# Recurrence of block 1 with two state tiles in turn and the modulation on column tiles, gate in the same block; attention's causal masks by VectorE

## What is computed

```
mod = silu(c) @ w_mod + b_mod                 # 1024 x 6144 weights; chunks 4 to 11 (of 512 columns) are needed later
# block 1, S5 mixer: a complex diagonal recurrence in both directions over 16 groups x 64 states
bul = einsum('btgp,gnp->btgn', ul, b_bar);  sl = s5_scan(bul.at[:, 0].add(a_bar * h0), a_bar)
y = gelu(real(einsum('gpn,btgn->btgp', c_mat, states)) + d_mat * u)
y_d = y * sigmoid(y @ glu_w + glu_b)
# block 2, attention: 8 heads of 64, causal, with a forget gate's cumulative sum c
logits = einsum('bhqd,bhkd->bhqk', q_i, kt) * scale + (c_i[:, :, :, None] - ck[:, :, None, :])
logits = where(kpos <= qpos, logits, -inf);  o = softmax(logits) @ v
```

## Time and profile before

| what | value |
|---|---|
| time, median of 3 runs (lowest, highest) | 2791.47 us (2787.81, 2792.29) |
| profiled execution: own time, span | 2791.35 us, 2789.6 us |
| mean granted clock of PE in the profiled execution | 0.929 of 2.4 GHz |
| busy share of the span: PE, DVE, ACT, POOL | 90%, 45%, 27%, 5% |
| DMA | 201 MB, mean 72 GB/s |

### The profile page before, as it was taken

One profiled execution on the slowest core, in us unless ns is written; L12 is line 12 of the kernel. 1 busy time (PEld: TensorE's weight loads), 2 busy tenths in 40 slices (PEclk: granted clock), 3 DMA queues, 4 the chain that ended last, 5 costly groups with the idle time before them and its releaser, 6 DMA issues. The chain is left out here.

```text
span 2789.6 us, 26647 instructions
## 1 busy us (share of the span) xinstructions
PE 2506.2 (90%) x11018; PEld 1828.3 (66%) x11018; DVE 1260.6 (45%) x1809; ACT 744.5 (27%) x1134; POOL 139.3 (5%) x125
## 2 busy tenths in 40 slices
PE   6999996777599999999999979997888998999799
PEld 2445861154577888778887858994566976454687
DVE  2775614523656443334443346416746175332410
ACT  1101110012023333223442243323425232233310
POOL 0000000002000000000000000005500000012000
PEclk9999997885599999999999999999999999799899
DMA  5540014300042333323333322100021211000431
GB/s 199 172 119 28 1 44 156 121 4 1 14 145 83 99 95 100 94 82 97 108 113 98 91 68 55 48 6 8 31 87 46 60 32 61 16 13 16 126 93 53
DMA packets 269697, 201.04 MB, mean 72 GB/s; under 512 B 17250, under 2 KB 250010, under 8 KB 268648
## 3 DMA queue, kind: packets, MB, share of 16 engines
q1 hardware_dynamic: 249800, 174.40, 20.5%
q10 hardware_dynamic: 16640, 14.68, 1.7%
q0 software_dynamic: 3136, 10.25, 1.0%
HBM read 173.69 MB, written 24.44 MB: 71 GB/s over the span
## 5 line engine op out<-in xcount | busy, mean ns | idle before, releaser
L1767 PE MATMUL bk_in<-h_part,w_part 128*128 128x512 f32 x2112 | 485.1, 392 | 9.5 <-DVE h_part L2056 6.7
L1767 PEld LDWEIGHTS bk_in<-h_part,w_part 128*128 128x128 f32 x2112 | 398.4, 189 | 95.5 <-DVE h_part L2056 7.1
L1854 ACT ACTIVATE w_part<-w_raw 128x1024 fp32r<-128x1024 f32 (+1 forms) x136 | 154.6, 1137 | 548.3 <-PE bk_in L1767 315.8
L1991 DVE TENSOR_TENSOR w_part<-w_raw,w_part 128x1024 fp32r<-128x1024 f32 (+1 forms) x136 | 179.3, 1319 | 227.1 <-ACT w_part L1854 227.0
L1767 PE MATMUL bk_out<-hid_part,w_part 128*128 128x512 f32 x1056 | 244.8, 394 | 7.6 <-DVE hid_part L2067 7.6
L1767 PEld LDWEIGHTS bk_out<-hid_part,w_part 128*128 128x128 f32 x1056 | 201.1, 191 | 51.1 <-DVE hid_part L2067 8.4
L3461 PE MATMUL fo_ps<-fo_hi,fo_part 128*128 128x512 f32 x512 | 161.9, 395 | 18.4 <-DVE fo_part L2215 18.4
L1022 PE MATMUL fr_ps<-arena,work 128*128 128x512 f32 x384 | 167.5, 598 | 0.1
L2326 PE MATMUL bk_in<-h_part,sj_part 128*128 128x512 f32 x576 | 135.3, 397 | 14.2 <-DVE h_part L2079 13.2
L2736 PE MATMUL aj_ps<-h_part,aj_part 128*128 128x512 f32 x576 | 137.8, 400 | 0.0
L2326 PEld LDWEIGHTS bk_in<-h_part,sj_part 128*128 128x128 f32 x576 | 109.9, 191 | 39.8 <-DVE h_part L2079 13.6
(11 more groups left out here) (553 smaller groups left out, 3473.9 us busy)
## 6 DMA issues: line engine op xcount, KB each, us to landing
w_raw<-in_w_ffn_in SPq DMA_DIRECT2D x88, 512.0 KB, 3.7
w_raw<-in_w_ffn_out SPq DMA_DIRECT2D x32, 704.0 KB, 4.4
work<-in_w_mod SPq DMA_DIRECT2D x16, 1024.0 KB, 5.2
work<-in_w_in SPq DMA_DIRECT2D x24, 512.0 KB, 3.6
w_raw<-in_w_in SPq DMA_DIRECT2D x20, 512.0 KB, 3.6
work<-in_w_mod ACTq DMA_DIRECT2D x4, 2048.0 KB, 21.6
w_raw<-in_w_out SPq DMA_DIRECT2D x16, 512.0 KB, 3.6
work<-in_w_out SPq DMA_DIRECT2D x8, 1024.0 KB, 7.0
```

Source lines behind the costliest of these rows:

```text
L1767: mm = pe.matmul(bank, w_part[:, n % 2, a, k, :], moving(b, k), start=(first and k == 0 and j == 0), stop=(last and k == kt - 1 and j == 2))
L1854: nc.scalar.activation(w_part[:, n % 2, 0, 0:kt, :], w_raw[:, n % 2, 0:kt, :], ACT.Copy)\
L1991: nc.vector.tensor_tensor(w_part[:, n % 2, 1, 0:kt, :], w_raw[:, n % 2, 0:kt, :], f32(w_part[:, n % 2, 0, 0:kt, :]), ALU.subtract).then_in ...
```

## The change

- In stage_s5 DVE takes two tiles in turn, real and imaginary part in one operation of 2 x 160 columns where their operands allow it, with the waits set two operations apart; PE makes the inputs of four tiles ahead (four banks `pv`) and issues the inputs of tile n + 4 behind modulation n.
- The modulation's product kk goes to column tile kk mod 3 (partitions 0, 32 or 64 of a bank of `pu`). ACT copies the three partial rows; `turn_row` is a matmul with `pick`, which adds them while it turns them, and is issued behind the odd tile's products of the next row. POOL clears the row buffers.
- The weights have four slots instead of two. Of the spilled data, `wvT` comes first; `K`, `ca` and the gate's weights come behind the first four slots, and PE waits for them before the outputs.
- The outputs of two groups alternate between the two halves of the partitions; the result is turned and copied in four steps; the gate follows in the same block, and stage_s5_glu and its entry in PHASES are gone.
- In stage_back PE waits for `rest` piece by piece in the first tile.
- In attention the mask matmuls are gone, and so is the identity in fp32r. DVE adds `late` (before the maximum) and `early` (before ACT's exponential, which waits for it) onto 128 columns in PSUM.

The diff, cut to its core; removed lines that only name the old views or repeat what is printed above are left out:

```diff
-    g_re, g_im, w1, w2 = (A.view(Z0 + 10 * T + 512 + i * NS, NS) for i in range(4))
+    g = [A.view(Z0 + 10 * T + 512 + i * 2 * NS, 2, NS) for i in range(2)]
+    w = [A.view(Z0 + 10 * T + 512 + (2 + i) * 2 * NS, 2, NS) for i in range(2)]
...
+    st = A.view(SV0, 2, DT, NS)
...
-    ring = [A.view(WR0 + i * 2 * T, HK, HALF) for i in range(2)]
-    rows = [A.view(H0 + 6 * T + i * HALF, HALF)[0:2, :] for i in range(2)]
+    ring = [A.view(at, HK, HALF) for at in (WR0, WR0 + 2 * T, C0, H0)]
+    M_ROWS = 66
+    rows = [A.view(H0 + 6 * T + i * HALF, HALF) for i in range(2)]
+    pick = A.view(H0 + 7 * T, 2)
+    gw = A.view(H0 + 7 * T + 16, 2, W_MIX)
+    sig = A.view(WR0, 2, T)
...
-        pv = psum(nc, ctx, "s6_v", 2, PSB)
-        po = psum(nc, ctx, "s6_o", 2, PSB)
-        pm = psum(nc, ctx, "s6_m", PSB)
+        pv = psum(nc, ctx, "s6_v", 4, PSB)
...
-                sp.dma_start(A.view(V.w_back, 6 * T), S.spill[:, V.N_CA:]).then_inc(s.back, 16)
+                sp.dma_start(A.view(V.w_back, 4 * T), S.spill[:, V.N_CA:V.N_CA + 4 * T]).then_inc(s.back, 16)
...
-                    if n >= 2:
-                        sp.wait_ge(m.done, n - 1)
+                    if n >= 4:
+                        sp.wait_ge(m.done, n - 3)
...
-                sp.dma_start(A.view(V.ca_back, V.N_CA), S.spill[:, 0:V.N_CA]).then_inc(s.back, 16)
-                for n in range(2, DT):
+                    sp.dma_start(ring[n % 4], w_mod[:, HK * (n % 2):HK * (n % 2) + HK, a:a + HALF])\
+                        .then_inc(loaded[n % 4], 16)
+                for n in range(4):
                     load(n)
+                sp.dma_start(A.view(V.w_back + 4 * T, 2 * T), S.spill[:, V.N_CA + 4 * T:]).then_inc(s.back2, 16)
+                sp.dma_start(A.view(V.ca_back, V.N_CA), S.spill[:, 0:V.N_CA]).then_inc(s.back2, 16)
...
+                    load(n)
+
+            @block.gpsimd
+            def _(pool):
+                for t in rows:
+                    pool.memset(t[0:M_ROWS, :], 0.0).then_inc(m.zero, 1)
+                pool.memset(pick[0:M_ROWS, :], 0.0).then_inc(m.zero, 1)
...
+                    pe.wait_ge(m.rowc, 3 * q + 3)
...
                         at = 2 * (4 * q + j)
-                        t = pe.transpose(pt[:, at:at + 2], rows[q % 2][:, j * P:(j + 1) * P], S.ident[0:2, 0:2])
+                        t = pe.matmul(pt[:, at:at + 2], rows[q % 2][0:M_ROWS, j * P:(j + 1) * P], pick[0:M_ROWS, :],
...
-                    if n >= 2 and n % 2 == 0:
...
+                    pe.wait_ge(loaded[n % 4], 16 * (n // 4) + 16)
                     for k in range(HK):
-                        mm = pe.matmul(pm[0:2, :], S.cs[:, HK * (n % 2) + k, :], ring[n % 2][:, k, :],
-                                       start=(n % 2 == 0 and k == 0), stop=(n % 2 == 1 and k == HK - 1))
+                        kk = HK * (n % 2) + k
+                        tile = 32 * (kk % 3)
+                        mm = pe.matmul(pu[tile:tile + 2, q % 2, :], S.cs[:, kk, :], ring[n % 4][:, k, :],
+                                       start=(kk < 3), stop=(kk >= KT - 3))
                     mm.then_inc(m.done, 1)
-
-                for g in range(S5G):
...
+                    if n % 2 and q:
+                        turn_row(q - 1)
...
+                def inputs(n):
+                    if n >= 4:
+                        pe.wait_ge(s.read, n - 3)
+                    d, t = n // KT, n % KT
+                    for ri in range(2):
+                        for e in range(2):
+                            mm = pe.matmul(pv[64 * e:64 * e + 64, n % 4, ri * NS:(ri + 1) * NS],
+                                           wvT[ri][:, n, 64 * e:64 * e + 64],
+                                           V.UT[:, 2 * t + e, S5CC * d:S5CC * d + NS], start=True, stop=True)
...
-                pe.wait_ge(s.back, 32)
+                pe.wait_ge(s.back, 16)
+                for n in range(4):
+                    inputs(n)
+                pe.wait_ge(m.pick, 3)
...
+                    modulation(n)
+                    if n + 4 < DT:
+                        inputs(n + 4)
+                turn_row(N_MOD - 1)
+                pe.wait_ge(s.back2, 32)
+                pe.wait_ge(s.table, 1)
...
+                def outputs(half):
+                    for i in range(4):
+                        groups = [8 * half + 2 * i + e for e in range(2)]
+                        o = [pv[:, 2 * half + e, i * P:(i + 1) * P] for e in range(2)]
...
-                    modulation(n)
...
+                            pe.matmul(o[e], V.UT[:, groups[e], S5CC:NS], K[:, groups[e], :], start=True, stop=False)
...
+                                for e in range(2):
+                                    part = slice(64 * e, 64 * e + 64)
+                                    mm = pe.matmul(o[e], st[part, ri, t, c0:c0 + S5C], ca[ri][part, t, first:first + P],
+                                                   start=False, stop=(d == 1 and ri == 1))
...
+                def turn_outputs(c):
+                    pe.wait_ge(s.gelu, 2 * c + 2)
+                    for b in range(2):
+                        if c:
+                            pe.wait_ge(s.ys, b + 1)
+                        for j in range(4):
+                            t = pe.transpose(pu[:, b, j * P:(j + 1) * P], V.yc[:, 4 * b + j, c * P:(c + 1) * P], S.ident)
+                        t.then_inc(s.turned2, 1)
...
+                outputs(0)
+                outputs(1)
+                turn_outputs(0)
+                turn_outputs(1)
+                pe.wait_ge(s.gw, 16)
+                pe.wait_ge(s.ys, 4)
+                for n in range(4):
+                    ch, h = n // 2, n % 2
+                    for k in range(2):
+                        mm = pe.matmul(pv[:, n, :], gw[:, k, ch * P:(ch + 1) * P], V.ys[:, k, h * HALF:(h + 1) * HALF],
+                                       start=(k == 0), stop=(k == 1))
+                    mm.then_inc(s.glu, 1)
...
+                act.wait_ge(m.zero, 3)
+                for j in range(3):
+                    part = slice(32 * j, 32 * j + 2)
+                    nc.scalar.activation(pick[part, :], S.ident[part, part], ACT.Copy).then_inc(m.pick, 1)
+                for q in range(N_MOD):
+                    act.wait_ge(m.done, 2 * q + 2)
+                    if q >= 2:
+                        act.wait_ge(m.turned, q - 1)
+                    for j in range(3):
+                        part = slice(32 * j, 32 * j + 2)
+                        nc.scalar.activation(rows[q % 2][part, :], pu[part, q % 2, :], ACT.Copy).then_inc(m.rowc, 1)
+                for half in range(2):
+                    act.wait_ge(s.out, half + 1)
+                    for e in range(2):
+                        g0 = 8 * half + e
+                        nc.scalar.activation(
+                            V.yc.rearrange("c j (g p) -> c g j p", g=S5G)[:, g0:g0 + 7:2, :, :],
+                            pv[:, 2 * half + e, :].rearrange("c (g j p) -> c g j p", g=4, j=S5L),
+                            ACT.Gelu_apprx_tanh).then_inc(s.gelu, 1)
...
+                    tim = [ti[:, n + i, :][:, way].unsqueeze(1).broadcast_to([P, 2, NS]) for i in range(2)]
+                    v = [pv[:, (n + i) % 4, 0:2 * NS].rearrange("p (r c) -> p r c", r=2) for i in range(2)]
+                    for i in range(2):
+                        dve.wait_ge(s.v, n + i + 1)
+                        nc.vector.tensor_tensor(g[i], v[i], tre[i], ALU.mult)
+                    for i in range(2):
+                        if n:
+                            dve.wait_ge(s.dve, done - 1 + i)
+                        nc.vector.tensor_tensor(w[i], v[i], tim[i], ALU.mult).then_inc(s.read, 1)
+                    for i in range(2):
+                        dve.wait_ge(s.read, n + i + 1)
+                        nc.vector.tensor_tensor(g[i][:, 0, :], g[i][:, 0, :], w[i][:, 1, :], ALU.subtract)
+                        nc.vector.tensor_tensor(g[i][:, 1, :], g[i][:, 1, :], w[i][:, 0, :], ALU.add)\
+                            .then_inc(s.dve, 1)
+                    for i in range(2):
+                        rate = r8[:, n + i:n + i + 1].broadcast_to([P, NS])
+                        dve.wait_ge(s.dve, done + i + 1)
+                        for ri in range(2):
+                            c = nc.vector.tensor_tensor_scan(g[i][:, ri, way], rate, g[i][:, ri, way], 0.0, ALU.mult,
+                                                             ALU.add)
+                        c.then_inc(s.dve, 1)
+                    for i in range(2):
+                        dve.wait_ge(s.dve, done + 2 + i + 1)
+                        nc.vector.tensor_tensor(w[i], g[i], tim[i], ALU.mult)
+                        nc.vector.tensor_tensor(st[:, :, n + i, :], g[i], tre[i], ALU.mult).then_inc(s.dve, 1)
+                    for i in range(2):
+                        dve.wait_ge(s.dve, done + 4 + i + 1)
```

(40 more changed lines are left out.)

180 lines of the change are left out of this document (44 added, 136 removed).

## The result

The changed kernel takes 2665.82 us (median of four runs, 2663.17 to 2668.74) against 2791.31 us for the kernel before in the same session: a ratio of 0.9553, 95% interval 0.9536 to 0.9569. Forecast were 2664 and a range of 2648 to 2705. The sum was right; in the profiled execution two of its terms were off by 9 us each, in opposite directions.

| part | forecast | measured | how |
|---|---|---|---|
| stage_s5 and gate | -96.6 | -105.8 | DVE's last product of the gate ends at 502.33 instead of 608.10 |
| `rest` | -6 | -6.9 | attention's first score matmul 112.7 earlier, less 105.8 |
| attention | -25 | -16.0 | from there to the next stage's first DMA 202.8 instead of 218.8 |
| stage_out (the stage behind attention) | 0 | +0.6 | the remainder |

What follows compares the result with a forecast made beforehand. PE, busy for 90% of the span, was taken as the bound, except in stage_s5 (a ring of PE and DVE waits) and before `rest`. Terms -96.6 (stage_s5 and gate), -6 (`rest`) and -25 (attention) sum to -127.6: 2664 us, range 2648 to 2705.

Steps and rivals of the forecast that it cites:

- `rest`: stage_back: PE starts on the first piece and follows DVE instead of waiting for all eight; -6 us (-4 to -7.5).
- DVE's pair: stage_s5 recurrence: DVE takes 6.94 us per pair of state tiles, eight pairs 55.5 us, from 422.4 to 477.9.
- PE beside it: stage_s5 recurrence: overlapping column tiles bring a modulation slot from 3.59 to 2.15 us, PE's pair to 6.7, close to DVE's.
- cold stretch: stage_s5 recurrence: PE short of weight slots before 440 runs cold matmuls at twice the time; 3 us added, outputs from 483.5.
- Outputs: end of stage_s5: two groups with row tiles in turn take 1.95 us, all sixteen 15.6 instead of 24.1.
- Attention, score masks: attention after its first 27 us: 0.89 us less PE work on each of 24 score units, 21.4 us.
- Attention, softmax masks: attention: 0.28 us less PE work on each of 32 softmax units, 9.0 us; 8.5 us of stalls booked back.
- Rival C: attention: PE, waiting in each unit, falls to 1.2 GHz and stays there, making the kernel slower, 2814 us; 2%.
- Rival B: attention gains nothing: DVE's additions, their waits and ACT form a chain as long as PE's old one; 2689 us; 20%.
- Rival A: recurrence: PE stays the bound, as column tiles don't overlap or PE runs at 1.2 GHz; 2678 to 2698 us; 15%.
- Rival D: recurrence: the ring stays, PE still waits for the row within the pair, eight pairs keep 16.8 us; 2732 us; 3%.
- the ring: stage_s5 before: PE waits for DVE's row copy, DVE for PE's next inputs; 16.8 us per pair, eight pairs some 130.

## Why the prediction was right, point by point

- **Start of the recurrence.** DVE's first operation came at 422.0, for a forecast of 422.4. Right.
- **DVE's pair.** It takes 6.61 us, for 6.94: the scans, taken at 0.455 us each, step by 0.39 when four stand in a row; the operations of 320 and 160 columns (0.40 and 0.24) were right. Eight pairs end at 475.6, not 477.9.
- **PE beside it.** The rule "the next tile's first pass runs beside the second" gave 2.15 us per slot; measured are 1.80, against 3.53 on one tile, so 1.96 times as fast. The Trainium skill (TensorE: Matmul & The Clock Gate, Part 3) has 2.38 times for three column tiles at 512 columns, by which a slot is estimated at 1.5 us. The trace lies between that and my rule. PE's pair is 2 x 1.80 + 2 x 0.70 + 0.98 = 6.0 us, under DVE's 6.6; I had 6.7, so that PE's last turn came at 480.5, behind DVE, and added 3 us for a cold stretch. The cold stretch came (clock 0.59 in the first window above). In the profiled execution of the changed kernel PE made up for it and was through with its last turn 0.3 us ahead of the first output, so outputs started at 475.8, not 483.5: 7.7 of the stage's 9.2 us. But that was close. In five of the eight profiled executions of this stage PE came 0.4 to 2.1 us behind DVE, the first outputs ran at half clock for 3 to 7 us, and the stage took 1.9 to 3.4 us longer. There the granted clock from 443 to 446 was 0.50 to 0.72, against 0.75 to 0.98 in the other three. So the size of the pair was wrong, and the worry about the cold stretch was not.
- **DMA.** Slot 4 came at 440.6, for 440. Right.
- **Outputs.** Two groups take 1.73 us as a mean, instead of 1.95, and all sixteen 13.8 instead of 15.6.
- **Turning and gate.** 12.7 us pass from the end of the outputs to the end of the stage; forecast were 12.4. Right.
- **`rest`.** 6.9 by the traces and 6.6 by its own run, for 6. Each of these is uncertain by some 3 to 5 us.
- **Attention, score masks.** 21.4 us were forecast on PE in the later part, and 22.9 measured. Right. The first phase was undersized: 3 forecast, 6.5 measured (first score matmul to first softmax matmul 20.75 us instead of 27.25). There the two forget-term matmuls of a unit, no longer broken up by a mask, run together.
- **Attention, softmax masks: the step that failed.** I took their 9.0 us off PE and booked 8.5 as stalls for both kinds together. The stalls were sized about right: PE's idle time grew by 9.6 us (8.5 to 18.1). But the 9.0 never appeared in its busy time, which stayed at 149.9 for 149.6 beside the score masks and rose to 176.4 from 172.5 without them. What I had put at nothing is the clock. An estimate from the windows of 1 us: taking half of the time at half clock off PE's busy time leaves 143.9 us with the score masks alone and 137.6 with both, 6 less; for the other pair it leaves 168.2 and 158.9, 9 less. So most of the 9 us did leave PE, and the longer stretches at half clock took them back. Rival C named this mechanism and gave it 2% as an all-or-nothing case; in part it was there. Rival B (DVE's and ACT's chain eats the gain) is right for this half of the edit and wrong for the other.
- **Attention, the ends.** There were two costs that I had not seen: the reciprocals queued behind the last additions (2.4 us), and ACT's table load of 1.28 us, which before lay in ACT's wait and now comes after it. From the first softmax matmul to the first exponential it takes 4.5 us, 3.2 with the softmax masks on PE.
- **Rival A** (PE the bound) is what the kernel becomes on one column tile, at 2685 inside its 2678 to 2698. **Rival D** (the ring stays) did not occur.

So the mechanism was right in the recurrence, for `rest` and for the score masks, and wrong for the softmax masks. That the total came within 2 us is luck: in the profiled execution 9 us of caution in the recurrence covered 9 us of masks that pay nothing.

## What to carry to other kernels

Before small work is moved off the busiest engine, look at who waits for it: the maximum after a score mask had time, the exponential after a softmax mask had not, and one half of this edit lost 8 of the 23 us that the other half won. When an instruction is added to an in-order queue, look at everything around it, the rare operations too: moving the reciprocals and the sums forward was worth 2 and 8 us. A pause of an engine beside the bound costs nothing only if that engine catches up before the two meet: here PE, 0.6 us faster per pair, did so in three profiled executions and missed it by up to 2 us in five. On the bound engine a pause is paid as idle time and often again as clock.

## What the runs showed of the hardware

- *A product order can hold or lose the clock.* The windows of the kernel with the outputs in the order of before, from the last turned row on:

```profile
474.00:476.00 2.00, 1.55 (x11) 1.38 (x12) 1.93 (x12) 1.38 (x2) 0.00 (x0) 1.00 0.00 0
476.00:478.00 2.00, 2.00 (x13) 1.76 (x14) 0.29 (x3) 0.00 (x0) 0.00 (x0) 0.89 0.00 0
478.00:480.00 2.00, 2.00 (x9) 1.57 (x8) 0.00 (x0) 0.00 (x0) 0.00 (x0) 0.50 0.00 0
...
485.00:500.00 15.00, 15.00 (x56) 12.53 (x57) 0.00 (x0) 1.08 (x2) 0.00 (x0) 0.50 0.00 0
```

  PE came out of pauses of 0.92 and 0.29 us, the clock fell to 1.2 GHz 2 us into the outputs, and it stayed there through the outputs, some 40 us of work without a pause. With a row tile per group it was the same. The same products with the row tiles in turn kept 1.00 in four profiles, and in six others the clock fell to 0.50 near their start and came back 3 to 7 us later. In the kernel with one tile at a time on DVE they start at half clock after a pause of 9.7 us, average 0.85 over the next 20, and step by 1.73 us per two groups again from 496 on. In the kernel before the serial order kept its 2.4 GHz. What tips it was not tried.
- *Busy work alone does not bring the clock back*: besides these outputs, attention with the softmax masks alone on DVE ran at 0.50 for the 22 us from 2398 to 2420 with PE busy throughout.
- *Three column tiles of two columns each*, float32 at 512 columns: 1.80 us for four products instead of 3.53, 1.96 times one tile. *Two row tiles in turn*, 64 rows, 128 columns: sixteen matmul instructions in 1.09 us, where eight on one tile take 1.08 (563.94 to 565.02 in the kernel before).
- *A DVE addition of 128 columns in PSUM* takes 0.29 us, and a maximum that reads its result starts 0.33 after it.
